# The token transform of 512 latents, folded about its middle: two table slabs per layer in place of four

## What is computed

```python
def fourier_mix(f):
    B, T, Cf = f.shape
    fg = f.astype(jnp.float32).reshape(B, T, FOURIER_GROUPS, Cf // FOURIER_GROUPS)
    out = jnp.fft.fft2(fg, axes=(1, 3), norm='ortho').real
    return out.reshape(B, T, Cf).astype(f.dtype)
```

## Time and profile before

| | us |
|---|---|
| median of 3 runs | 1658.15 |
| lowest and highest | 1657.6, 1663.88 |
| profiled execution, own time | 1669.98 |
| its span in the profile | 1668.1 |
| PE busy | 1600.2 |
| DVE busy | 905.4 |
| POOL busy | 893.1 |
| ACT busy | 326.7 |

### The profile page before, as it was taken

How to read it: one execution, slowest core, us unless ns; L and a number is a source line. 1 busy time by engine, 2 the same in 40 slices (tenths; PEclk the granted TensorE clock), 3 DMA queues, 4 the chain that set the end, 5 groups by cost and what they waited for, 6 DMA issues and landing times.

```text
span 1668.1 us, 24031 instructions
## 1 busy us (share of the span) xinstructions
PE 1600.2 (96%) x8780; PEld 1328.9 (80%) x8780; DVE 905.4 (54%) x1310; ACT 326.7 (20%) x489; POOL 893.1 (54%) x846
## 2 busy tenths in 40 slices
PE   8999899989899999999999998998999999999997
PEld 2778788878788888888888887877877788888886
DVE  2697544376778865784277626635543542242343
ACT  2512111231321200221022214121231320120221
POOL 1156333385355465554455442554466677777774
PEclk9999999999899999999999998999999999999999
DMA  8245111243143343332334222331223232323322
GB/s 347 91 162 170 45 41 50 73 152 106 60 141 109 119 158 101 126 126 76 99 117 131 82 76 70 107 92 61 64 76 101 76 99 90 101 97 105 101 88 101
DMA packets 49644, 174.52 MB, mean 105 GB/s; under 512 B 6449, under 2 KB 6833, under 8 KB 48561
## 3 DMA queue, kind: packets, MB, share of 16 engines
q1 hardware_dynamic: 45504, 167.79, 30.1%
q10 hardware_dynamic: 4080, 5.94, 1.3%
HBM read 167.41 MB, written 2.10 MB: 102 GB/s over the span
## 4 chain that ended last, share of the span: by engine, by line
PE 72%; DVE 17%; issue 5%; ACT 2%; POOL 1%; DMA 1%; DVEq 1%; ACTq 1%; SPq 0%; POOLq 0%
PE pair L1020 63%; DVE aux L631 3%; DVE tg L962 2%; PE pair L1073 2%; DVE tv L962 2%; DVE h_lo L736 1%; DVE nt L720 1%; DVE hid_lo L990 1%; PE aux L1232 1%; DVE tv L987 1%; POOL w_lo L401 1%; ACT hid_hi L609 1%; PE aux L1202 1%; PE aux L1290 1%; ACT tv L601 1%
## 5 line engine op out<-in xcount | busy, mean ns | idle before, releaser
L399 POOL TENSOR_SCALAR w_hi<-raw 128x512 fp32r<-128x512 f32 (+1 forms) x420 | 298.7, 711 | 719.0 <-PE pair L1020 628.9
L401 POOL TENSOR_TENSOR w_lo<-raw,w_hi 128x512 fp32r<-128x512 f32 (+1 forms) x420 | 596.0, 1419 | 35.1
L1020 PE MATMUL pair<-h_hi,w_hi 128*128 128x512 f32 x1888 | 572.3, 361 | 11.6 <-POOL w_lo L401 7.2
L1020 PE MATMUL pair<-h_lo,w_hi 128*128 128x512 f32 x1888 | 567.0, 358 | 11.1 <-DVE h_lo L736 9.3
L1020 PE MATMUL pair<-h_hi,w_lo 128*128 128x512 f32 x1888 | 563.0, 356 | 0.0
L1020 PEld LDWEIGHTS pair<-h_lo,w_hi 128*128 128x128 f32 x1888 | 310.4, 190 | 73.2 <-DVE h_lo L736 18.4
L1020 PEld LDWEIGHTS pair<-h_hi,w_hi 128*128 128x128 f32 x1888 | 311.7, 191 | 69.1 <-issue 12.0
L1020 PEld LDWEIGHTS pair<-h_hi,w_lo 128*128 128x128 f32 x1888 | 311.0, 190 | 51.7
L631 DVE CUSTOM_DVE_ANT_0 aux<-mod_slot,c_b 128x1024 f32<-128x1024 f32 x160 | 227.3, 1420 | 7.1 <-DMA mod_slot<-in_mods 4.0
L926 DVE SCALAR_TENSOR_TENSOR x<-pair,modv,x 128x256 f32 (+3 forms) x96 | 60.6, 659 | 217.5 <-PE pair L1020 217.4
L1020 PE MATMUL pair<-hid_hi,w_hi 128*128 128x512 f32 (+1 forms) x528 | 161.2, 360 | 5.0 <-ACT hid_hi L609 5.0
(11 more groups left out here) (136 smaller groups left out, 1006.0 us busy)
## 6 DMA issues: line engine op xcount, KB each, us to landing
raw<-in_slabs SPq DMA_DIRECT2D x210, 512.0 KB, 3.4
mod_slot<-in_mods SPq DMA_DIRECT2D x80, 512.0 KB, 3.5
start_slot<-in_start_mods SPq DMA_DIRECT2D x8, 1024.0 KB, 13.5
x<-in_x SPq DMA_DIRECT2D x4, 768.0 KB, 18.1
rot<-kT ACTq DMA_DIRECT2D x32, 64.0 KB, 2.1
rot<-Y ACTq DMA_DIRECT2D x32, 64.0 KB, 2.2
out<-fin SPq DMA_DIRECT2D x8, 256.0 KB, 2.1
c_b<-in_c SPq DMA_DIRECT2D x1, 512.0 KB, 4.0
```

What stands on the lines that cost most here:

```text
L399: nc.gpsimd.tensor_scalar(w_hi[p][:, a:b], raw[p][:, a:b], 1.0, 1.0, ALU.mult, ALU.mult).then_inc(split, 1)
L401: nc.gpsimd.tensor_tensor(w_lo[p][:, a:b], raw[p][:, a:b], w_hi[p][:, a:b].bitcast(fp32), ALU.subtract).then_inc(split, 1)
L1020: ins = nc.tensor.matmul(out[:, a:b], wt, xt[:, a:b], start=first and k == 0, stop=last and k == 2)
```

## The change

A transform over T = 512 tokens with cosines is the same for token t and T - t, and with sines it is opposite. So the kernel now folds the tokens first: for t from 1 to 255 it takes f[t] + f[T - t] for the cosine part (in place in `Y`) and f[t] - f[T - t] for the sine part (in `ct`), with token 0 standing alone. That leaves 256 tokens, two chunks, for the sums. Token 256, the middle, has only a cosine part, +1 or -1 by the parity of the output token; it is added when the result is evicted.

- `NLF = 2` latent slabs per layer are streamed and used in place of `NLC = 4`; the context's two slabs in layer 0 are as they were.
- DVE gets `fold(b)` for both blocks: a memset of one column, a subtraction and an addition of 255 columns, one operand of each read backwards. They stand after the last tile of the first gate slab.
- `channels(n)` for latent chunks is now two matmuls of 128 columns for each block (even part with cosines, odd part with sines) in place of one of 256.
- Two matmuls of one column each put the channel transform of the middle token into two columns of `pair[0]`. They are issued in step n = 1 of the transform and wait until the gate slab in that bank is drained.
- DVE copies the middle to `mid`, and evicts the latent result with a scalar_tensor_tensor (sign x middle + sum) in place of a copy. TensorE waits for `mid_ready` before the output projection.
- `G_hi` and `G_lo` have a chunk of their own for every step, so ACT no longer waits for a chunk to be read.
- High and low parts of y are made inside the loop only from step n = 2 on. In layer 1, which now has two steps, all of them come after it; in DVE's order all eight low parts stand after the eviction.

```diff
+NLF = NLC // 2
 def dft_slabs(layer):
-    return NLC + (NCC if layer == 0 else 0)
+    return NLF + (NCC if layer == 0 else 0)
...
+    middle = pair[0][:, 1022:1024]
...
                 for n in range(dft_slabs(l)):
                     act.wait_ge(s["G_done"], n + 1)
-                    if n >= NLC:
-                        act.wait_ge(done, PLAN[l, "dft"] + n - NLC + 1)
-                    nc.scalar.activation(G_hi[:, n % NLC, :], aux(n % 2), ACT.Copy).then_inc(s["G_hi_ready"], 1)
+                    nc.scalar.activation(G_hi[:, n, :], aux(n % 2), ACT.Copy).then_inc(s["G_hi_ready"], 1)
                     if n < 2:
                         gate(2 + n)
-                    elif n >= dft_slabs(l) - 2:
-                        output_hi(Y_ORDER[n - dft_slabs(l) + 2])
-                for k in Y_ORDER[2:]:
+                    else:
+                        output_hi(Y_ORDER[n - 2])
+                for k in Y_ORDER[dft_slabs(l) - 2:]:
                     output_hi(k)
...
+                def fold(b):
+
+                    f, odd, h = Y[:, 4 + b, 0:T], ct[:, b * T // 2:(b + 1) * T // 2], T // 2
+                    dve.wait_ge(*drained_by(PLAN[l, "cbf"] + 2 * b + 1))
+                    chain(nc.vector.memset(odd[:, 0:1], 0.0))
+                    chain(nc.vector.tensor_tensor(odd[:, 1:h], f[:, 1:h], f[:, T - 1:h:-1], ALU.subtract))
+                    chain(nc.vector.tensor_tensor(f[:, 1:h], f[:, 1:h], f[:, T - 1:h:-1], ALU.add))
+
...
                         if k == KB - 1 and phase == "g" and j == 0:
                             while conv_due:
                                 convolution(conv_due.pop(0))
+                            dve.wait_ge(s["conv_done"], FB)
+                            for b in range(FB):
+                                fold(b)
...
                     if n < 2:
                         gated(2 + n)
-                    elif n >= dft_slabs(l) - 2:
-                        output_lo(n - dft_slabs(l) + 2)
-                    if n == dft_slabs(l) - 1:
-
-                        parts = [(NLC, 0, T)] + ([(NLC + NCC, T, TC)] if l == 0 else [])
-                        for count, a0, a1 in parts:
-                            dve.wait_ge(done, PLAN[l, "dft"] + count)
-                            for b in range(FB):
-                                src = aux(2 + b)[:, 0:T] if a0 == 0 else aux(0)[:, b * C:b * C + C]
-                                nc.vector.tensor_copy(Y[:, 4 + b, a0:a1], src).then_inc(s["four_ready"], 1)
-                for n in range(2, KB):
+                    else:
+                        output_lo(n - 2)
+                dve.wait_ge(done, PLAN[l, "dft"] + NLF)
+                nc.vector.tensor_copy(mid[:, :], middle).then_inc(s["mid_ready"], 1)
+                dve.wait_ge(s["mid_ready"], 1)
+                for b in range(FB):
+                    nc.vector.scalar_tensor_tensor(
+                        Y[:, 4 + b, 0:T].rearrange("p (t s) -> p t s", s=2),
+                        small[:, 4:6].unsqueeze(1).to_broadcast([P, T // 2, 2]), mid[:, b:b + 1],
+                        aux(2 + b).rearrange("p (t s) -> p t s", s=2), ALU.mult, ALU.add).then_inc(s["four_ready"], 1)
+                if l == 0:
+                    dve.wait_ge(done, PLAN[l, "dft"] + NLF + NCC)
+                    for b in range(FB):
+                        nc.vector.tensor_copy(Y[:, 4 + b, T:TC], aux(0)[:, b * C:b * C + C])\
+                            .then_inc(s["four_ready"], 1)
+                for n in range(dft_slabs(l) - 2, KB):
                     output_lo(n)
...
                     for b in range(FB):
-                        ins = nc.tensor.matmul(aux(n % 2)[:, b * 2 * P:(b + 1) * 2 * P], Y[:, 4 + b, col:col + CH],
-                                               chan[:, :], start=True, stop=True)
+                        if n < NLF:
+                            even, odd = Y[:, 4 + b, n * P:n * P + P], ct[:, b * T // 2 + n * P:b * T // 2 + n * P + P]
+                            nc.tensor.matmul(bank[:, 2 * b * P:(2 * b + 1) * P], even, chan[:, 0:P],
+                                             start=True, stop=True)
+                            ins = nc.tensor.matmul(bank[:, (2 * b + 1) * P:(2 * b + 2) * P], odd, chan[:, P:2 * P],
+                                                   start=True, stop=True)
...
+                    if n == 1:
+                        pe.wait_ge(*drained_by(PLAN[l, "g"] + 2))
+                        for b in range(FB):
+                            nc.tensor.matmul(middle[:, b:b + 1], chan[:, 0:P], Y[:, 4 + b, T // 2:T // 2 + 1],
+                                             start=True, stop=True)
...
+                pe.wait_ge(s["mid_ready"], 1)
                 slabs_into_norm(PLAN[l, "out"], Y_ORDER, h_hi, h_lo, cols, parts_ready(s["y_hi"], s["y_split"], 1),
...
-        slabs.append(token_tables(T))
+        slabs.append(token_tables(T)[:NLF])
```

More of the change, by code:

```diff
@@ L75, in narrow @@
 def narrow(s):
-    return PLAN[0, "dft"] + NLC <= s < PLAN[0, "dft"] + NLC + NCC
+    return PLAN[0, "dft"] + NLF <= s < PLAN[0, "dft"] + NLF + NCC
 def pair_uses(s):
@@ L164, in build_program @@
     chan = new("chan", [P, 2 * P])
-    small = new("small", [P, 4])
+    small = new("small", [P, 6])
     eps = new("eps", [P, 1])
@@ L182, in build_program @@
     c_cols = new("c_cols", [P, KB, 2])
+    mid = new("mid", [P, FB])
     rs = new("rs", [P, 8])
@@ L270, in build_program @@
     for l in range(DEPTH):
-        names = ["decay_exp", "decay_ready", "roped", "tr_done", "v_moved", "k_moved", "conv_done", "vz_ready",
+        names = ["decay_exp", "decay_ready", "roped", "tr_done", "v_moved", "k_moved", "conv_done", "mid_ready", "vz_ready",
                  "u_done", "state_ready", "qxi_ready", "scores_done", "St_ready", "o_done", "o_copied", "osq_ready",
@@ L411, in _ @@
             act.dma_start(c_cols[:, :, :], io["c_cols"]).then_inc(c_cols_loaded, 16)
-            for dst, src in ((vecs[:, :], io["vecs"]), (ident[:, :], tab[:, 1792:1920]), (small[:, :], tab[:, 2176:2180])):
+            for dst, src in ((vecs[:, :], io["vecs"]), (ident[:, :], tab[:, 1792:1920]), (small[:, :], tab[:, 2176:2182])):
                 act.dma_start(dst, src).then_inc(first_loaded, 16)
@@ L887, in _ @@
                     dve.wait_ge(s["G_hi_ready"], n + 1)
-                    nc.vector.tensor_tensor(G_lo[:, n % NLC, :], aux(n % 2), G_hi[:, n % NLC, :].bitcast(fp32),
+                    nc.vector.tensor_tensor(G_lo[:, n, :], aux(n % 2), G_hi[:, n, :].bitcast(fp32),
                                             ALU.subtract).then_inc(s["G_split"], 1)
@@ L1264, in channels @@
                         pe.wait_ge(s["G_split"], n - 1)
-                    col = n * CH
+                    bank = aux(n % 2)
                     for b in range(FB):
-                        ins = nc.tensor.matmul(aux(n % 2)[:, b * 2 * P:(b + 1) * 2 * P], Y[:, 4 + b, col:col + CH],
-                                               chan[:, :], start=True, stop=True)
+                        if n < NLF:
[4 more added lines that the diff above has]
+                                                   start=True, stop=True)
+                        else:
+                            col = T + (n - NLF) * P
+                            ins = nc.tensor.matmul(bank[:, b * 2 * P:(b + 1) * 2 * P], Y[:, 4 + b, col:col + P],
+                                                   chan[:, :], start=True, stop=True)
                     ins.then_inc(s["G_done"], 1)
@@ L1278, in _ @@
                     sl, p = PLAN[l, "dft"] + n, n % 2
-                    w = T if n < NLC else C
+                    w = T if n < NLF else C
                     pe.wait_ge(split, 4 * sl + 2)
                     pe.wait_ge(s["G_split"], n + 1)
-                    first, last = n in (0, NLC), n in (NLC - 1, nd - 1)
+                    first, last = n in (0, NLF), n in (NLF - 1, nd - 1)
+                    if n == 1:
[3 more added lines that the diff above has]
+                                             start=True, stop=True)
                     for t in range(2):
-                        if t and n < NLC:
+                        if t and n < NLF:
                             pe.wait_ge(split, 4 * sl + 4)
@@ L1288, in _ @@
                             for k, (G, W) in enumerate(((G_hi, w_hi), (G_lo, w_hi), (G_hi, w_lo))):
-                                if n < NLC:
-                                    ins = nc.tensor.matmul(aux(2 + b)[:, 0:w], G[:, n % NLC, g],
+                                if n < NLF:
+                                    ins = nc.tensor.matmul(aux(2 + b)[:, 0:w], G[:, n, g],
                                                            W[p][:, t * w:(t + 1) * w], start=first and t == 0 and k == 0,
@@ L1293, in _ @@
                                 else:
-                                    ins = nc.tensor.matmul(aux(0)[:, b * w:(b + 1) * w], G[:, n % NLC, g],
```

(4 more changed lines are left out.)

## The result

| | before | changed |
|---|---|---|
| median of 5 runs, us | 1662.18 | 1650.63 |
| lowest and highest | 1657.6, 1664.27 | 1644.98, 1652.01 |
| span of the profiled execution | 1668.1 | 1644.1 |
| granted clock over the span | 0.978 | 0.981 |

The ratio is 0.9917, 95% interval 0.9896 to 0.9938: of 1662.18 that is 13.8 us less, between 10.3 and 17.3 (the plain difference of the two medians is 11.6). The prediction was 12.4 us less. The two intervals share only their ends; the forecast lies between them. As a time, 1650.63 us lies inside the forecast range and 4.8 us above the 1645.8 forecast; 4.0 of these are the base, since before's median was 1658.15 over the three runs known then and is 1662.18 over five.

The account below looks back on a forecast made before the run. TensorE is busy 96%, but POOL's half slabs bound layer 0's transform; in layer 1 TensorE, then DVE. 8.3 - 0.7 + 4.8 = 12.4 us saved, from 1658.15 to 1645.8 us, range 1641.0 to 1652.2.

Parts of the forecast that it names:

- POOL sets layer 0: Layer 0, transform to projection: POOL's half slabs are the path; four of nine go, saving 8.3 us, bounds 7.7 to 9.9.
- the fifth half slab: Layer 0, the projection's first half on POOL: meets DVE's remaining low parts, 2.75 us, between 1.96 and 3.39.
- The second and fourth: Layer 0, two of POOL's five remaining half slabs: each meets a low part on DVE, 2.75 us each.
- The slow clock stays: Layer 0 projection: idle wait stays about 3.9 us, so the slow clock's 2.4 us cost over seven blocks stands.
- the rival: Layer 0 projection: the slow clock goes, another 2.4 us gained, 14.8 saved, 1643.4 us; chance 0.15.
- The fold: Six DVE instructions per layer: 3.7 us taken in layer 0, costing TensorE 0.7 (0 to 1.7); covered in layer 1.
- The covers of 3.0 and 5.1 us: Fold time on DVE that costs TensorE nothing: up to 3.0 us in layer 0, 5.1 in layer 1.
- The rival in which the fold turns the change into a loss: Both layers: slow reversed reads make DVE stall TensorE; break-even at F = 10.6 us, 1670 at F = 16.5; chance 0.03.
- DVE sets layer 1: Layer 1 projection: TensorE waits for DVE's low parts after the evictions; seventh block at 1240.5, 4.8 us saved, bounds 2.9 to 7.0.
- the forecast waits before blocks 6 and 7: Layer 1 projection: TensorE waits for low parts 6 and 7, which meet POOL's splits and end at 1240.1.
- the second rival: Layer 1: all moved low parts meet POOL, TensorE's clock falls, 2.4 us lost; 6.5 saved in all, 1651.7 us; chance 0.18.
- the forecast's own signs of being wrong: Fold operations far above 0.42 us, a late first raw slab of the projection, or the clock falling in layer 1.

Follow-up runs that it names:

- e9: The changed kernel measured once more, unaltered, in a later series: 0.9943 of before, 9.5 us less.
- e2: The change applied in layer 0 alone, layer 1 as in the kernel before: 0.9938 of before, 10.3 us less.
- e6: The changed kernel with the fold moved behind the next masked scores in both layers: 0.9908 of before.
- e7: The changed kernel with three low parts of y in layer 1 made before DVE waits for the transform's end: 0.9912 of before.
- e10: The changed kernel with two low parts of y in layer 1 made before DVE waits for the transform's end: 0.9936 of before.
- e5: The changed kernel with the fold's six instructions run four times over: 1.0024 of before, 4.0 us slower than before.
- e1: The kernel before, making one product of three in latent slabs 2 and 3, all slabs still split: 0.9985 of before, 2.5 us less.
- e8: The changed kernel with POOL splitting 8 instead of 512 columns of each context slab's unused half: 0.9895 of before.

## Why the prediction was right

- *POOL sets layer 0.* Right. It was forecast that 8.3 us go between the first table product and the projection; 9.4 went. The term that was mis-sized is the fifth half slab: 2.75 assumed, 1.97 measured, because DVE was then at the evictions, which read PSUM, and its six low parts began only at 335.94. The second and fourth were 0.2 each too dear. The sum of the five was forecast at 13.2 us and is 12.0.
- *The slow clock stays.* Right in the profile after (10.13 us for seven blocks), but that is the extreme. In the six other profiles with the same wait (2.75 to 2.77 us) the seven blocks took 8.94 (e9), 9.03 (e2), 9.00 (e6), 9.01 (e7), 8.82 (e10) and 7.72 (e5). So it usually costs some 1.5 us and not 2.4, and once, in e5, the rival came true at the full wait. The earlier trace rows show only the clock's fall; its return is in the profile after, at 342.9. e1 and e8 keep the clock in the projection and take 7.80 and 8.31.
- *The fold.* 3.7 us forecast, 3.27 measured; its cost 0.7 forecast, 0.38 measured. A reversed read costs nothing: 0.42 us as the earlier trace rows. The covers of 3.0 and 5.1 us are confirmed by e5. The rival in which the fold turns the change into a loss was worked out at F = 10.6 us; e5 has this F, and it is 4.0 us slower than before, where the break-even was put. The clock after each wait, which that rival left out, goes the right way; the difference was not taken apart further.
- *DVE sets layer 1.* Right for the start, not for the end: 4.8 forecast, 5.75 and (with e9) 5.9 measured. The projection starts 0.45 us earlier than worked out, and eight low parts take 6.84 us where 7.5 was given for seven (1232.65 to 1240.1), since POOL's next half slab came only at 1217.21, when six were done. So DVE was done early, the forecast waits before blocks 6 and 7 never came, and TensorE ran 1.35 us behind low part 7. What held it was the clock (0.56 from 1213.0 to 1216.5), as the second rival had it and as one of the forecast's own signs of being wrong. Without it the eighth block could have begun about 1217.6, 1.3 us earlier, if POOL's splits had stayed where they are (an estimate from the rows above); e10, with the full clock, shows that they don't, and takes 15.12 us. Two errors here go against each other, which is luck.
- The Trainium skill's rule (SBUF — State Buffer, "SBUF: two separate sides") would spare an operation that reads PSUM and one SBUF operand. The four new evictions (they also take one number per partition, `mid`) last 0.740 to 0.747 us, all beside POOL: this agrees.

```profile
L913 DVE SCALAR_TENSOR_TENSOR Y<-small,mid,aux x4: 740/744/747, 333.9 to 1210.9; 128x512 f32<-128x512 f32 x4
```

By the stages the change is worth 9.1 + 5.75 - 0.4 = 14.5 us in its first profile and 10.3 + 5.9 - 0.4 = 15.8 in e9's. Both savings were forecast too small and the fold's cost too large, so that 12.4 lies between the measured 9.5 and 13.8 is in part luck. What stays open is why the last series shows 9.5 and the first 13.8, and why it shows less than its stages. The variants that can't be told from the changed kernel go with their series, e6 and e7 at 0.9908 and 0.9912, e10 beside e9 at 0.9936, so the series may matter more than the kernel; that is not shown.

## What to carry to other kernels

Before costing matmuls that a change removes, look at what released the stage behind them: here 9.4 of some 14.5 us were those of the engine that prepares the weights, and removing two thirds of the same matmuls with the splits kept gave 2.5 us of 14. When two engines contend, work moved into one's idle time can take away the other's gap, so an early start may return nothing. And a wait of TensorE can have a second price, the slow clock after it, which has to stand in the sum as a range: after the same wait of 2.75 to 2.77 us seven blocks took from 7.72 to 10.13 us, and in layer 1 the clock fell after waits of 0.25 and 1.35 us.

## What the runs showed of the hardware that was not expected

In the layer-0 MLP the matmul pairs of 512 and 256 columns stand either 0.347 or 0.353 us apart on average, through a hundred us and more, at a granted clock of 1.00 in both cases. It is no property of the kernel: the changed kernel has both, first its first profile, then e9.

```profile
500.18 0.51 PE L1040 MATMUL pair<-h_hi,w_hi 128*128 128x512 f32 x2
500.52 0.51 PE L1040 MATMUL pair<-h_hi,w_lo 128*128 128x512 f32 x2
```

```profile
499.68 0.51 PE L1040 MATMUL pair<-h_hi,w_hi 128*128 128x512 f32 x2
500.03 0.52 PE L1040 MATMUL pair<-h_hi,w_lo 128*128 128x512 f32 x2
```

Four profiles, the changed kernel's first, e2's, e6's and e10's, have 0.347 nearly throughout. e9 and most others have 0.353 up to about 570 us and 0.347 from about 630 on; before and e1 keep 0.353 to about 760. For before's some 240 us at the longer spacing, 0.0066 in 0.35 makes between 4 and 5 us (an estimate), of the 7.1 by which the stretch between the two stages differs. It may be one reason why a single pair of profiles differs by 24 us where the ratios give 9.5 and 13.8; that was not measured by itself.
